# Second retention head in block form, with the token sums made on VectorE during the first head's output product

## The reference

```python
def mixer_layer(x, pos, S0, ...):
    xn = rmsnorm(x, ln_g)
    proj = xn @ w_in                                   # 1024 -> q, k, v, z_a, x_b, z_b, g_a, g_b
    q = rope(q.reshape(B, L, RET_HEADS, RET_DK), pos)  # 4 heads of 256
    k = rope(k.reshape(B, L, RET_HEADS, RET_DK), pos) * (RET_DK ** -0.5)
    v = v.reshape(B, L, RET_HEADS, RET_DV)             # 4 heads of 512
    ret, S_new = retention(q, k, v, ...)
    o_a = group_norm(ret, gn_g) * silu(z_a)
    ...                                                # RG-LRU branch o_b
    merged = sigmoid(g_a) * (o_a @ w_a) + sigmoid(g_b) * (o_b @ w_b)
    return x + merged @ w_o, S_new, conv_new, h_last
```

## Time and profile before

| what | value |
|---|---|
| three runs | 1884.08, 1881.15, 1881.06 us, median 1881.15 us |
| the profiled execution | 1882.79 us |
| its span (first to last instruction) | 1881.0 us, so 1.8 us lie outside it |
| busy: PE, PEld, DVE, ACT, POOL | 99%, 93%, 73%, 46%, 17% of the span |
| head 1, layer 0, from its first projection matmul to its last output matmul | 147.18 to 278.72 us |
| head 2, layer 0, likewise | 278.72 to 407.34 us |

### The profile page before, as it was taken

How to read it: one execution, slowest core, us unless ns; L and a number is a source line. 1 busy time by engine, 2 the same in 40 slices (tenths; PEclk the granted TensorE clock), 3 DMA queues, 4 the chain that set the end, 5 groups by cost and what they waited for, 6 DMA issues and landing times.

```text
span 1881.0 us, 32869 instructions
## 1 busy us (share of the span) xinstructions
PE 1862.7 (99%) x12908; PEld 1744.2 (93%) x12908; DVE 1379.2 (73%) x2338; ACT 871.3 (46%) x1440; POOL 325.2 (17%) x457
## 2 busy tenths in 40 slices
PE   8999999999999999999999999999999999999998
PEld 8899898898899999999998988988989999999997
DVE  7777677677766877866897776777867578878575
ACT  5432334433437776542444323434333377766334
POOL 2221130130231210100132211203102422001010
PEclk9999999999999999999999999999999999999999
DMA  6436565575453333543755455754843533327253
GB/s 221 137 119 220 173 212 163 167 226 181 142 155 91 105 98 98 156 133 101 204 175 162 143 176 177 226 166 153 283 135 129 167 102 106 101 85 185 96 164 113
DMA packets 131479, 289.10 MB, mean 154 GB/s; under 512 B 13790, under 2 KB 54222, under 8 KB 131198
## 3 DMA queue, kind: packets, MB, share of 16 engines
q1 hardware_dynamic: 93710, 166.23, 28.8%
q0 software_dynamic: 37472, 120.78, 21.0%
q10 hardware_dynamic: 144, 0.00, 0.0%
HBM read 223.29 MB, written 53.97 MB: 147 GB/s over the span
## 4 chain that ended last, share of the span: by engine, by line
PE 86%; DVE 4%; DMA 3%; ACT 3%; DVEq 1%; issue 1%; ACTq 1%; SPq 0%
PE bank L2669 17%; PE bank L2671 17%; PE bank L2670 17%; PE bank L2763 4%; PE bank L2764 4%; PE bank L2765 4%; PE bank L2780 4%; PE bank L2782 4%; PE bank L2783 4%; DMA w_raw<-in_w_units 2%; PE sums L2839 1%; PE sums L2763 1%; PE sums L2765 1%; PE sums L2764 1%; PE sums L2964 1%
## 5 line engine op out<-in xcount | busy, mean ns | idle before, releaser
L2669 PE MATMUL bank<-xn_hi,w_hi 128*128 128x296 f32 (+1 forms) x1760 | 527.2, 300 | 1.8 <-DVE acc L2597 0.8
L2671 PE MATMUL bank<-xn_lo,w_hi 128*128 128x296 f32 (+1 forms) x1760 | 522.7, 297 | 0.0
L2670 PE MATMUL bank<-xn_hi,w_lo 128*128 128x296 f32 (+1 forms) x1760 | 522.1, 297 | 0.0
L2669 PEld LDWEIGHTS bank<-xn_hi,w_hi 128*128 128x128 f32 x1760 | 330.9, 188 | 8.9 <-issue 6.3
L2670 PEld LDWEIGHTS bank<-xn_hi,w_lo 128*128 128x128 f32 x1760 | 331.3, 188 | 0.9
L2671 PEld LDWEIGHTS bank<-xn_lo,w_hi 128*128 128x128 f32 x1760 | 330.6, 188 | 0.0
L732 DVE TENSOR_TENSOR w_lo<-w_raw,w_hi 128x1024 fp32r<-128x1024 f32 x203 | 248.8, 1229 | 69.2 <-ACT w_hi L722 64.4
L722 ACT ACTIVATE w_hi<-w_raw 128x1024 fp32r<-128x1024 f32 x203 | 212.3, 1054 | 177.6 <-DMA w_raw<-in_w_units 174.0
L2669 PE MATMUL bank<-oa_hi,w_hi 128*128 128x296 f32 (+1 forms) x512 | 153.7, 300 | 0.0
L2670 PE MATMUL bank<-oa_hi,w_lo 128*128 128x296 f32 (+1 forms) x512 | 151.9, 297 | 0.0
L2671 PE MATMUL bank<-oa_lo,w_hi 128*128 128x296 f32 (+1 forms) x512 | 151.7, 296 | 0.0
(11 more groups left out here) (376 smaller groups left out, 4270.0 us busy)
## 6 DMA issues: line engine op xcount, KB each, us to landing
w_raw<-in_w_units SPq DMA_DIRECT2D x173, 512.0 KB, 3.6
w_raw<-in_w_units SPq DMA_DIRECT2D x199, 256.0 KB, 4.3
S<-in_state_ret POOLq DMA_DIRECT2D x64, 512.0 KB, 5.0
out_ret_s<-S POOLq DMA_DIRECT2D x64, 512.0 KB, 6.2
sum_raw<-sum_scr POOLq DMA_DIRECT2D x16, 592.0 KB, 11.0
w_raw<-in_w_units POOLq DMA_DIRECT2D x32, 256.0 KB, 4.4
sum_scr<-sum_raw POOLq DMA_DIRECT2D x8, 592.0 KB, 4.8
vst<-v_scr SPq DMA_DIRECT2D x8, 512.0 KB, 3.8
```

Of the source, the lines that this page charges most:

```text
L2669: pe.matmul(ps, w_hi[:, slot, cols], x_hi, start=first, stop=False)
L2670: pe.matmul(ps, w_lo[:, slot, cols], x_hi, start=False, stop=False)
L2671: return pe.matmul(ps, w_hi[:, slot, cols], x_lo, start=False, stop=last)
```

## The change

`PAIR_HEADS` becomes `(1, 2, 3)`: head 1 makes its queries and keys in block form too. With it:

- All of `token_sum` is made in head 0's output product, in one go, and it no longer works in place: the four quarters of the tokens go to planes 4 to 7 (`RAW11`, `RAW12`, `RAW22`, `RAW21`), the four sums to planes 0 to 3. ACT's high halves later overwrite the quarters.
- In head 0's output product DVE no longer empties the banks; ACT does (`first_taken`), with the high halves of sums and parts between the copies.
- POOL stores each raw sum as soon as it is made (`store_sum`), among the adds for head 1's parts, and ahead of the state stores; all three adds of that place (keys' `S1`, queries' `S1`, keys' `S3`) now stand ahead of the state stores. DVE's `sum_low` overwrites a raw sum in place, so for head 1 it waits until that sum's store has landed. The `sums_out` waits in head 1 are gone.
- SP loads 14 half-unit parts for head 1's queries and keys in place of four units.

```diff
-PAIR_HEADS = (2, 3)
+PAIR_HEADS = (1, 2, 3)
...
+                def store_sum(n):
+
+                    pool.wait_ge(right_ready, l * READIES + n + 1)
+                    if l:
+                        pool.wait_ge(again_in[n], (l - 1) * AGAIN + 16 * len(PAIR_HEADS))
+                    pool.dma_start(sum_scr[n], sum_raw[:, n, :, :].rearrange("p k t -> p (k t)")).then_inc(again_in[n], 16)
...
-                    if h + 1 in PAIR_HEADS:
+                    if h + 1 == PAIR_HEADS[0]:
+                        keys, queries = head_pairs(h + 1)
+                        store_sum(DIFF)
+                        add_part(keys, S1)
+                        store_sum(MIX2)
+                        store_sum(EDGE)
+                        store_sum(LAST)
+                        add_part(queries, S1)
+                        add_part(keys, S3)
+                    elif h + 1 in PAIR_HEADS:
                         load_sums(h)
...
+                    def first_taken(two, n):
+
+                        a, b = cut(l)[n]
+                        for m in (2 * two, 2 * two + 1):
+                            name = (("wa", m), n)
+                            wait_job(act, "R", l, h, name)
+                            act.activation(acc[:, m, a:b], psum_of("R", name)[:, 0:b - a], ACT.Copy)\
+                               .then_inc(freed("R", name), 1)
...
+                        first_taken(2, 0)
+                        high_sum(DIFF)
+                        part_high(keys, A11)
+                        first_taken(2, 1)
+                        high_sum(MIX2)
+                        high_sum(EDGE)
+                        first_taken(3, 0)
+                        part_high(keys, S1)
+                        split_hi(act, "R", l, h, 14)
+                        high_sum(LAST)
+                        part_high(keys, S2)
+                        first_taken(3, 1)
+                        split_hi(act, "R", l, h, 15)
+                        part_high(keys, A12)
...
                 def sum_low(h, n):
 
+                    if h == PAIR_HEADS[0]:
+                        dve.wait_ge(again_in[n], l * AGAIN + 16)
                     right_low(SUMS * PAIR_HEADS.index(h) + n + 1, sum_lohi[:, n, :, :], plane(n), sum_lohi[:, SUMS + n, :, :])
...
+                    if h + 1 == PAIR_HEADS[0]:
+                        grow_four(0)
+                        split_lo(dve, "R", l, h, 12)
+                        token_sum(DIFF)
+                        token_sum(MIX2)
+                        token_sum(EDGE)
+                        token_sum(LAST)
+                        split_lo(dve, "R", l, h, 13)
+                        grow_four(1)
+                        part_low(keys, A11)
+                        sum_low(h + 1, DIFF)
+                        part_add(keys, S2, S1)
+                        part_low(keys, S1)
+                        sum_low(h + 1, MIX2)
+                        split_lo(dve, "R", l, h, 14)
+                        part_add(keys, S4, S2)
+                        part_low(keys, S2)
+                        split_lo(dve, "R", l, h, 15)
+                        part_low(keys, A12)
+                        sum_low(h + 1, EDGE)
```

More of the change, by code:

```diff
@@ L1773, in plane, with tokens @@
                     return sum_raw[:, n, :, :]
[L1775 removed]
+                def tokens(n):
+                    to, k, half = TOKENS[n]
                     a, b = HALVES[half]
                     dve.tensor_tensor(plane(to), xn_hi[:, k:k + 4, a:b].bitcast(f32), xn_lo[:, k:k + 4, a:b].bitcast(f32), ADD)
[L1779 to L1799 removed]
@@ new lines, in _ @@
+                    if h + 1 == PAIR_HEADS[0]:
+                        grow_four(0)
[17 more added lines that the diff above has]
+                        sum_low(h + 1, EDGE)
+                    else:
+                        for two in range(KT // 2):
+                            taken_up(two, 0)
+                            if two % 2 == 0:
+                                grow_four(two // 2)
+                            taken_up(two, 1)
+                            split_lo(dve, "R", l, h, 12 + two)
+                            if h + 1 in PAIR_HEADS:
+                                if two == 1:
+                                    sum_low(h + 1, DIFF)
+                                    sum_low(h + 1, MIX2)
+                                elif two == 2:
+                                    part_low(keys, A11)
+                                    part_add(keys, S2, S1)
+                                    part_low(keys, S1)
+                                elif two == 3:
+                                    part_add(keys, S4, S2)
+                                    part_low(keys, S2)
+                                    part_low(keys, A12)
+                                    sum_low(h + 1, EDGE)
```

142 lines of the change are left out of this document (58 added, 84 removed).

## The result

The changed kernel takes **1887.93 us** (median of 12 runs, 1883.66 to 1892.9) against 1882.15 us before (12 runs, 1879.43 to 1885.85); the ratio is 1.0031, 95% interval 1.0021 to 1.004. It is 0.3% slower, where 1875.5 us was forecast. The profiled execution took 1887.94 us, its span is 1886.1 us.

What follows compares the result with a forecast made beforehand. PE, busy 99% of the span, was taken as the bound; head 1's blocks at 23.1 us save 2.98 and 2.70 us, together 5.7 off the median 1881.15, giving 1875.5 us, range 1873.8 to 1879.2.

Steps and rivals of the forecast that it cites:

- the paragraph on the state stores: POOL's row before head 1's block: stores wait behind the keys' `S3` add, until about 26.5 instead of 20.0 us; PE unaffected.
- its 5 us of room: Head 1's queries' `S3`: by head 2's spacing, the part is due some 5 us after its add lands.
- The rule: Block form's keys' half: PE's wait is about the `S3` add's landing, counted from the block's start, less 4.8 us.
- the other end, 6.5: Keys' `S3` add of head 1 taking 6.5 us, not 4.2: lands up to 6.1 us in, costs 1.3 us.
- The sums' stores: POOL's raw-sum stores in head 0's product: 5.4 us each, landed at about 25 us, zero cost to PE.
- the queue rule of the Trainium skill: DMA engines alternate between queues packet by packet; so state stores in the add's own ring made 6.5 us of 4.2.
- SP's loads at zero: Head 1's 14 part loads replace four units; DMA shares 0.74 to 0.78 against 0.75 and 0.77, so zero cost.
- Blocks that wait as heads 2 and 3 do: Rival: head 1's blocks take 23.67 us each, 4.5 us off, 1876.6 us; chance 0.21.
- The slower one: Rival: a late sum store holds DVE, PE waits 3.5 us, the clock falls, some 1.5 us; 1885.2 us; chance 0.06.
- DVE's chain: Head 0's output product: DVE busy from 4.4 to 30.8 us, narrowest margin 1.9 us at `S2`, no cost to PE.
- ACT's bank copies at zero: Head 0's output product: sixteen copies, 6.7 us of ACT's 16 in 27.35; banks emptied in time, zero cost.
- PE's gain: Head 1's queries and keys: 24 matmuls fewer a layer, blocks 23.1 us, together 5.7 us off.

Runs made afterwards that it cites:

- the kernel with the late state loads: Against the kernel with all three adds ahead of the state stores: heads 1 to 3 load the next states behind the queries' last product; 1877.1 us, ratio to before 0.9968.
- the `S1` add behind: Changed kernel, with POOL issuing the add for the queries' `S1` behind that for the keys' `S3` in head 0; 1886.04 us, ratio to before 1.0025.
- state stores behind both adds: Changed kernel, with both `S3` adds of head 1 ahead of all four state stores; 1884.96 us, ratio to before 1.0011.
- the same order in heads 2 and 3: Changed kernel, with the keys' `S3` add ahead of the state stores in heads 2 and 3 as well; 1893.63 us, ratio to before 1.0062.

## Why the prediction was wrong

**The step that failed** is the paragraph on the state stores: "Nothing of PE waits for them: the next is POOL's add for the queries' `S3`, which may be issued about 2 us later than in head 2". I moved the stores 6 us in POOL's row and counted their issue, not their landing. POOL waits for that landing one instruction ahead of the queries' add. In head 2 the wait was free, since the stores had left 14.7 us before the add; here the add came 7 us later than there, and its 5 us of room were gone. The profile puts 4.0 us of loss in layer 0's queries' half and a wait of 0.6 us in layer 1 behind it. With the add ahead of that wait, and nothing else changed, these losses went to 0 and 0.3 us, and the time fell by 6 us (by the two ratios, 5). That this whole fall is the wait's is not shown, since the keys' half, which stands ahead of the edit, differs by over 4 us between executions of the same row.

**The keys' `S3`, mis-sized.** The rule held: landings at 5.57 and 7.55 us less 4.8 give 0.8 and 2.75 us, and the fifth product began 0.5 and 2.5 us late (7.10 and 9.08 us in, against 6.56); the clock cost another 1.5 us in layer 1. What failed are the terms: for the load I took 4.3 and it took 5.86 and 7.16; for the add 4.2, and it took 5.75 and 6.29, near the other end, 6.5, that I had kept for the range; with the load of 7.16 the landing in layer 1 lies beyond even that end (6.1). The sums' stores had landed at 25 us as I counted, but the queries' `S1` add 1 us ahead of the load was not weighed at all. On the queue rule of the Trainium skill that I weighed there ("DMA: Bandwidth & Descriptors", section "Queues, rings and completion order"): the keys' `S3` add of head 1 took 3.6 to 7.3 us without a state store ahead of it in its queue, and 8.6 in both layers behind four of them. So without a state store ahead it already spreads over the whole of my range, and what the own queue adds to that these runs do not separate. The sum had no ground to choose the low end, and the trace of before held an add that I did not read, for the queries' `S1` of head 2, issued at 261.30 us behind four loads of sums and no state store (KB, us to landing):

```profile
rot<-in_w_units POOLq DMA_DIRECT2D x1, 256.0 KB, 6.9
```

**SP's loads at zero.** I compared DMA shares (0.74 to 0.79 in the rows, where I wrote 0.78); a mean share does not show how late one load comes. A values' unit load of 10.22 us cost 2.4 us in layer 1. The trace of before had loads as long in head 1 (8.35 and 9.89 us behind its state loads), where the direct form had no need of them so soon.

**The rivals.** Blocks that wait as heads 2 and 3 do was the nearer mechanism for the keys' half. The slower one named the wrong cause (no sum's store held DVE), but its last link, the clock falling behind a wait at 1.5 us, came about in layer 1. No rival had POOL's wait in it. That alone is not why the range missed: with the wait out of the way the time is 1881.78 us, still above the range's end of 1879.2.

**What was right.** DVE's chain: the last token step ended 19.2 us after the first output matmul (forecast 19.6), the `EDGE` low half at 31.1 (30.8), and PE waited for no sum. ACT's bank copies at zero. The sums' stores: 5.1 to 6.8 us in layer 0 (5.4). PE's gain: with the causes away, in the kernel with the late state loads (which changes heads 2 and 3 too), the blocks take 23.16 and 23.65 us (23.1), and by its ratio the time is 6.0 us under the kernel before (5.7).

## What to carry to other kernels

When an instruction is moved in an in-order queue, go on down the queue to the next wait on its completion and ask what stands behind that wait; the cost of a move lies there, not at the place moved to. Put transfers that nobody waits for (here 2 MB of stores) behind the small ones that someone does, and in no case ahead of a wait that these share. A duration of a DMA from one place in the program holds only beside the same traffic: count the bytes issued within a few microseconds of it, and even then take a range: the same add behind the same row of POOL took 4.3 to 7.3 us in layer 1.

## What the runs showed of the hardware

- The DMA engines are busy all the time in a part of this block. From 153 to 157 us of the changed kernel (the last two numbers are the DMA share and GB/s):

```profile
153.00:157.00 4.00, 3.58 (x25) 3.18 (x25) 3.23 (x5) 3.02 (x6) 0.00 (x0) 1.00 1.04 413
```

  Between the keys' add and the stores' landing (147.33 to 161.01) 3.93 MB moved; at 413 GB/s that alone would be 9.5 us of the 13.7, an estimate from these two numbers. It is the rate of this mix of transfers: from 164 to 167 us the engines were as busy (1.02) at 236 GB/s. The Trainium skill, "DMA: Bandwidth & Descriptors", section "Specifications", gives 435 GB/s as the fabric's ceiling and some 358 GB/s as one core's share of the memory; 413 lies under the first and over the second.
- A wait of 2.3 us was followed by a product at half clock in one layer, one of 2.2 us in the other layer by none. The length does not tell them apart: in the other profiles such a spell came with waits of 1.75 us (the `S1` add behind, layer 0) and 1.83 us (state stores behind both adds, layer 0), and none with one of 2.75 us (the same order in heads 2 and 3, layer 0). What does, these runs do not show.
- The same load of half a values' unit, 0.2 us behind the same first state load, took 4.9 to 6.2 us in four blocks of the changed kernel's profile and 10.2 in a fifth; in the sixth it left 0.3 us ahead of the state loads and took 5.0. Why is open.
